# Hybrid decoder trunk: the stationary activation tiles stored interleaved, with gaps between the tensors

## The reference

```python
h = h + gated_deltanet(rms_norm(h, ...), gdn_w_in, gdn_conv_w, ..., gdn_w_out)   # 2048 -> 12352 -> 2048
h = h + swiglu_ffn(rms_norm(h, ...), w_gate_up, w_down)                          # 2048 -> 2 x 5632 -> 2048
shared_kv = nsa_shared_kv(h, kv_norm_g, kv_w, ...)                               # 2048 -> 3072
h = h + nsa_attention(rms_norm(h, ...), shared_kv, w_in, w_out)                  # 2048 -> 2096, 2048 -> 2048
h = h + swiglu_ffn(rms_norm(h, ...), w_gate_up, w_down)
return rms_norm(h, final_norm_g)
```

## Time and profile before

| | |
|---|---|
| time, median of three | 2800.06 us |
| profiled execution | 2803.94 us |
| its span | 2802.1 us |
| granted clock of TensorE, mean | 0.995 |
| PE busy | 2739.6 us, 13456 matmuls |
| weight loads busy | 2282.1 us, 13456 |
| DVE busy | 2219.6 us |
| ACT busy | 1648.4 us |
| read from HBM | 489.86 MB, 176 GB/s over the span |

### The profile page before, as it was taken

The page is one execution under the profiler, slowest core; times in us unless marked ns, Lnnn a source line. Parts: engine busy times, 40 slices in busy tenths (PEclk is TensorE's granted clock), DMA queues, the critical chain, the costliest instruction groups (busy, mean ns, idle before and its releaser), DMA issues.

```text
span 2802.1 us, 40252 instructions
## 1 busy us (share of the span) xinstructions
PE 2739.6 (98%) x13456; PEld 2282.1 (81%) x13456; DVE 2219.6 (79%) x2727; ACT 1648.4 (59%) x2184; POOL 31.0 (1%) x30
## 2 busy tenths in 40 slices
PE   8999999999988999999999999999999999999998
PEld 6878888888877888888888888888887888888887
DVE  5867877878767788888888876557677888888887
ACT  6766767667665555555555555554555555555554
POOL 0000000000000000000000000000000000000000
PEclk9999999999999999999999999999999999999999
DMA  6534444445433566656666656643345666656664
GB/s 239 181 124 153 159 144 163 156 149 167 158 105 113 166 210 199 198 185 203 198 198 203 198 172 224 222 135 114 106 158 188 207 199 200 199 184 200 198 201 166
DMA packets 135097, 493.23 MB, mean 176 GB/s; under 512 B 15009, under 2 KB 15329, under 8 KB 134625
## 3 DMA queue, kind: packets, MB, share of 16 engines
q1 hardware_dynamic: 133776, 487.82, 52.8%
q10 hardware_dynamic: 1232, 4.23, 0.4%
HBM read 489.86 MB, written 2.13 MB: 176 GB/s over the span
## 4 chain that ended last, share of the span: by engine, by line
PE 65%; issue 29%; DVE 3%; ACT 2%; DMA 1%; POOL 0%; POOLq 0%; DVEq 0%; SPq 0%; ACTq 0%
PE ACC L733 10%; PE ACC L735 10%; PE ACC L734 10%; PE SIDE L943 7%; PE SIDE L944 7%; PE SIDE L945 7%; PE ACC L943 3%; PE ACC L944 3%; PE ACC L945 3%; PE SIDE L741 2%; DVE W_LO L1627 1%; DMA RAW<-stream 1%; PE SIDE L1138 1%; ACT W_HI L1194 0%; ACT WORK L1587 0%
## 5 line engine op out<-in xcount | busy, mean ns | idle before, releaser
L1627 DVE TENSOR_TENSOR W_LO<-RAW,W_HI 128x1024 fp32r<-128x1024 f32 x424 | 511.6, 1222 | 268.9 <-ACT W_HI L1194 265.8
L1194 ACT ACTIVATE W_HI<-RAW 128x1024 fp32r<-128x1024 f32 x424 | 443.3, 1057 | 217.5 <-PE ACC L735 183.8
L1436 ACT ACTIVATE W_HI<-WORK 128x1024 fp32r<-128x1024 f32 x320 | 325.4, 1031 | 345.8 <-PE SIDE L945 232.7
L733 PE MATMUL ACC<-W_HI,X_HI 128*128 128x512 f32 x1216 | 491.2, 404 | 17.7 <-DVE W_LO L1627 17.6
L735 PE MATMUL ACC<-W_HI,X_LO 128*128 128x512 f32 x1216 | 477.6, 393 | 0.0
L734 PE MATMUL ACC<-W_LO,X_HI 128*128 128x512 f32 x1216 | 476.7, 392 | 0.0
L1878 DVE TENSOR_TENSOR W_LO<-WORK,W_HI 128x1024 fp32r<-128x1024 f32 x300 | 364.5, 1221 | 119.0 <-ACT W_HI L1436 116.3
L1436 ACT ACTIVATE W_HI<-RAW 128x1024 fp32r<-128x1024 f32 x328 | 314.8, 980 | 237.0 <-PE ACC L735 141.6
L733 PE MATMUL ACC<-W_HI,A_HI 128*128 128x512 f32 x928 | 370.3, 399 | 0.7 <-issue 0.7
L735 PE MATMUL ACC<-W_HI,A_LO 128*128 128x512 f32 x928 | 362.7, 391 | 0.0
L734 PE MATMUL ACC<-W_LO,A_HI 128*128 128x512 f32 x928 | 362.2, 390 | 0.0
(11 more groups left out here) (363 smaller groups left out, 3798.7 us busy)
## 6 DMA issues: line engine op xcount, KB each, us to landing
RAW<-stream SPq DMA_DIRECT2D x752, 512.0 KB, 4.6
WORK<-stream SPq DMA_DIRECT2D x160, 512.0 KB, 4.8
WORK<-gdn_rows ACTq DMA_DIRECT2D x8, 512.0 KB, 6.2
WORK<-xt SPq DMA_DIRECT2D x4, 512.0 KB, 9.3
H<-x SPq DMA_DIRECT2D x2, 1024.0 KB, 13.6
out<-WORK SPq DMA_DIRECT2D x4, 512.0 KB, 3.5
WORK<-tails SPq DMA_DIRECT2D x2, 512.0 KB, 10.8
WORK<-gfin SPq DMA_DIRECT2D x1, 1024.0 KB, 6.6
```

Source lines behind the costliest of these rows:

```text
L733: nc.tensor.matmul(dst, hi[:, at:at + P], wh, start=first and h % 2 == 0 and q == 0, stop=False)
L1194: nc.scalar.activation(W_HI[:, h % WS, :], raw_piece(h), ACT.Copy).then_inc(hi_ready, 1)
L1436: nc.scalar.activation(dst, src, ACT.Copy).then_inc(hi_ready, 1)
L1627: nc.vector.tensor_tensor(W_LO[:, h % WS, :], raw_piece(h), W_HI[:, h % WS, :].bitcast(f32), SUB).then_inc(lo_ready, 1)
```

## The change

The two token tiles of a k-tile are stored interleaved: column 2i + t of the 256 columns of a k-tile holds token i of token tile t. A stationary tile is then 128 words at a step of two. All that write such tiles (ACT for the high part, DVE for the low part) write with a step of two and read the transposed source in its old order; DVE reads the high part with a step of two. The tail matmuls read X as the moving operand in two runs with a step of two, so that their output has the old order. The token sums read X in the new order and write contiguous tiles as before.

Three unused tensors of 16 words (64 bytes per partition) lie before A_HI, before B_HI and after H. X then starts at a multiple of 4 KB from the weights W_HI and W_LO, A at 64 bytes more, B and H at 128 bytes more, and TR and all that follows at 192 bytes more. The scaled form of `act_in_vector` becomes two operations, one for each token tile.

```diff
@@ build: the tensors in SBUF
-        A_HI, A_LO, B_HI, B_LO = (sb(n, [P, CHK * SEQ], f32r) for n in ("A_HI", "A_LO", "B_HI", "B_LO"))
+        sb("GAP_A", [P, 16])
+        A_HI, A_LO = (sb(n, [P, CHK * SEQ], f32r) for n in ("A_HI", "A_LO"))
+        sb("GAP_B", [P, 16])
+        B_HI, B_LO = (sb(n, [P, CHK * SEQ], f32r) for n in ("B_HI", "B_LO"))
         H = sb("H", [P, NT, DM])
+        sb("GAP_Z", [P, 16])
@@ new helpers
+        def paired(ap):
+            return ap.rearrange("p (u i t) -> p u t i", t=NT, i=P)
+        def plain(ap):
+            return ap.rearrange("p (u t i) -> p u t i", t=NT, i=P)
+        def stationary(buf, at):
+            first = at // SEQ * SEQ + at % SEQ // P
+            return buf[:, first:first + SEQ - 1:NT]
@@ products (up_products and last_products likewise)
-                    nc.tensor.matmul(dst, hi[:, at:at + P], wh, start=first and h % 2 == 0 and q == 0, stop=False)
-                    nc.tensor.matmul(dst, hi[:, at:at + P], wl, start=False, stop=False)
-                    m = nc.tensor.matmul(dst, lo[:, at:at + P], wh, start=False, stop=last and h % 2 == 1 and q == 1)
+                    x_hi_, x_lo_ = stationary(hi, at), stationary(lo, at)
+                    nc.tensor.matmul(dst, x_hi_, wh, start=first and h % 2 == 0 and q == 0, stop=False)
+                    nc.tensor.matmul(dst, x_hi_, wl, start=False, stop=False)
+                    m = nc.tensor.matmul(dst, x_lo_, wh, start=False, stop=last and h % 2 == 1 and q == 1)
@@ tail_tensor
-                nc.tensor.matmul(SIDE[0][:, 0:SEQ], both, X_HI[:, at], start=kt == 0, stop=False)
-                m = nc.tensor.matmul(SIDE[0][:, 0:SEQ], both, X_LO[:, at], start=False, stop=kt == KT - 1)
+                dst = plain(SIDE[0][:, 0:SEQ])
+                nc.tensor.matmul(dst, both, paired(X_HI[:, at]), start=kt == 0, stop=False)
+                m = nc.tensor.matmul(dst, both, paired(X_LO[:, at]), start=False, stop=kt == KT - 1)
@@ norm_scalar (first_scalar, act_in_scalar and the casts of hid_t likewise)
-                i = nc.scalar.activation(X_HI[:, kt * SEQ:(kt + 1) * SEQ], SIDE[r % 2][:, q * SEQ:(q + 1) * SEQ],
+                i = nc.scalar.activation(paired(X_HI[:, kt * SEQ:(kt + 1) * SEQ]),
+                                         plain(SIDE[r % 2][:, q * SEQ:(q + 1) * SEQ]),
@@ norm_vector (first_vector and hid_lo likewise)
-                i = nc.vector.scalar_tensor_tensor(X_LO[:, at], SIDE[r % 2][:, q * SEQ:(q + 1) * SEQ],
+                i = nc.vector.scalar_tensor_tensor(paired(X_LO[:, at]), plain(SIDE[r % 2][:, q * SEQ:(q + 1) * SEQ]),
...
-                                                   X_HI[:, at].bitcast(f32), MUL, SUB)
+                                                   paired(X_HI[:, at].bitcast(f32)), MUL, SUB)
@@ act_in_vector
-            hi = to_hi[:, :].bitcast(f32)
+            hi, lo, full = paired(to_hi[:, :].bitcast(f32)), paired(to_lo[:, :]), plain(SIDE[p][:, :])
             if gain is None:
-                i = nc.vector.tensor_tensor(to_lo[:, :], SIDE[p][:, :], hi, SUB)
+                i = nc.vector.tensor_tensor(lo, full, hi, SUB)
             else:
-                i = nc.vector.scalar_tensor_tensor(to_lo[:, :], SIDE[p][:, :], gain, hi, MUL, SUB)
+                for t in range(NT):
+                    i = nc.vector.scalar_tensor_tensor(lo[:, :, t, :], full[:, :, t, :], gain, hi[:, :, t, :], MUL, SUB)
@@ token_sums
-            x4 = x_sum.rearrange("p (j a n) -> p a j n", j=4, a=4)
-            a11, a21, a12, a22 = (x4[:, i] for i in range(4))
+            x4 = x_sum.rearrange("p (j q n t) -> p q t j n", j=4, q=2, t=NT)
+            a11, a21, a12, a22 = (x4[:, q, t] for q in range(2) for t in range(NT))
```

More of the change, by code:

```diff
@@ L953, in up_products @@
             kt = 4 * j + (2 if kind[0] == "p" else 0)
-            a11, a21, a12, a22 = (tuple(b[:, at:at + P] for b in (X_HI, X_LO))
+            a11, a21, a12, a22 = (tuple(stationary(b, at) for b in (X_HI, X_LO))
                                   for at in ((kt + q) * SEQ + t * P for q in range(2) for t in range(NT)))
@@ L982, in last_products @@
                         wh, wl = (b[:, h % WS, q * COLS:(q + 1) * COLS] for b in (W_HI, W_LO))
-                        m = three(dst, B_HI[:, at:at + P], B_LO[:, at:at + P], wh, wl, h == 30 and q == 0, h == 31 and q == 1)
+                        m = three(dst, stationary(B_HI, at), stationary(B_LO, at), wh, wl, h == 30 and q == 0, h == 31 and q == 1)
                     if t:
@@ L1221, in first_scalar @@
                 at = slice(kt * SEQ, (kt + 1) * SEQ)
-                i = nc.scalar.activation(X_HI[:, at], XT[:, at], ACT.Copy, scale=PRM[:, A_GAIN + kt:A_GAIN + kt + 1])
+                i = nc.scalar.activation(paired(X_HI[:, at]), plain(XT[:, at]), ACT.Copy, scale=PRM[:, A_GAIN + kt:A_GAIN + kt + 1])
             i.then_inc(x_hi, 1)
@@ L1239, in act_in_scalar @@
             act.wait_ge(side_full[p], n)
-            nc.scalar.activation((to or A_HI)[:, :], SIDE[p][:, :], ACT.Copy, scale=gain).then_inc(act_hi, 1)
+            nc.scalar.activation(paired((to or A_HI)[:, :]), plain(SIDE[p][:, :]), ACT.Copy, scale=gain).then_inc(act_hi, 1)
         def pairs64(buf):
@@ L1476, in ffn_scalar @@
                     act.wait_ge(side_out[0], ph.after("hid_t", 0))
-                    nc.scalar.activation(A_HI[:, :], hid_t, ACT.Copy).then_inc(act_hi, 1)
+                    nc.scalar.activation(paired(A_HI[:, :]), plain(hid_t), ACT.Copy).then_inc(act_hi, 1)
             for k in range(0 if first else 4):
@@ L1486, in ffn_scalar @@
                         act.wait_ge(side_out[0], ph.after("hid_t", it))
-                        nc.scalar.activation(B_HI[:, :], hid_t, ACT.Copy).then_inc(act_hi, 1)
+                        nc.scalar.activation(paired(B_HI[:, :]), plain(hid_t), ACT.Copy).then_inc(act_hi, 1)
                 for half in range(2):
@@ L1633, in first_vector @@
                 at = slice(kt * SEQ, (kt + 1) * SEQ)
-                i = nc.vector.scalar_tensor_tensor(X_LO[:, at], XT[:, at], PRM[:, A_GAIN + kt:A_GAIN + kt + 1],
-                                                   X_HI[:, at].bitcast(f32), MUL, SUB)
+                i = nc.vector.scalar_tensor_tensor(paired(X_LO[:, at]), plain(XT[:, at]),
+                                                   PRM[:, A_GAIN + kt:A_GAIN + kt + 1],
+                                                   paired(X_HI[:, at].bitcast(f32)), MUL, SUB)
             i.then_inc(x_first, 1)
@@ L1955, in hid_lo @@
                 dve.wait_ge(act_hi, n + hi0)
-                nc.vector.tensor_tensor(lo[:, :], hid_t, hi[:, :].bitcast(f32), SUB).then_inc(act_lo, 1)
+                nc.vector.tensor_tensor(paired(lo[:, :]), plain(hid_t), paired(hi[:, :].bitcast(f32)), SUB).then_inc(act_lo, 1)
             for e in range(0 if first or final_ else 24):
```

## The result

The kernel with the change takes 2854.75 us (median of 4, 2854.14 to 2857.69) beside 2800.29 for the kernel before on the same chip (4 runs, 2799.73 to 2801.63). The ratio is 1.0196, with a 95% interval from 1.0178 to 1.0214: slower by 2.0%, 54.5 us. The prediction said 2714 us and faster.

The account below looks back on a forecast made before the run. PE was taken as the bound: number of matmuls times step. From 2803.9 us (profiled execution), minus 89 for the shorter step, plus 3 for strided operations and tail, came 2718; against the median 2714 us, range 2685 to 2915.

Parts of the forecast that it names:

- What the step is made of: Each 512-column fp32r matmul: 226.8 ns were 213.3 of streaming plus the moving words' read stream meeting the weight load's.
- Part (1): Stationary tiles of X, A, B at every second word: 9552 matmuls step at 216 ns, saving 89 us, 76 to 103.
- The end of 213.3: Lower limit of the step of the 9552 matmuls with strided stationary tiles: it can't go below 213.3 ns.
- The end of 237.9: Upper limit of that step: the load may fetch twice as many pieces, doubling the excess of 11.1 to 237.9 ns.
- arriving share: How much step saving reaches the span: all 49 us in FFN, three quarters of 54 us elsewhere, 40 us.
- Part (2): ACT and DVE writing X, A, B, and DVE reading the high half, at every second word: 2 us, ends 0 and 8.
- Part (3): Scaled split of the attention input as two operations of 512 elements: 747 each against 1278, +0.22 us eight times; nothing.
- Part (4): The 64 matmuls of 256 columns at L769/L770 stream X at every second word: 1 us, from 0 to 7.
- Part (5): The three gaps shifting A by 64 bytes, B and H by 128, what follows by 192: put at nothing.
- twice the collisions: Rival at each of the 9552 steps: load collides twice as often, step 237.9 ns, +106 us, 2909; chance 0.23.
- The distance decides: Rival: X at distance 0 keeps its step, 2769 (chance 0.09), or collides permanently, 2840 (0.06); the other tiles gain.
- no change: Rival: the excess is sequencing between load and matmul that doesn't see addresses; 2803 us, chance 0.10.

Follow-up runs that it names:

- the streams: No kernel computation: segments of 48 identical matmuls on one core, stationary tile contiguous or at every second word, at various distances from W; 590.76 us in all.

## Why the prediction was wrong, point by point

*What bounds the kernel*: right. The steps of PE times their count give what was measured.

*What the step is made of*: here the prediction failed, before any edit was priced. It read 226.8 ns as 213.3 of streaming plus collisions with the load, which end when the two streams advance equally fast, and took L901 and L793 for signs of it. L901 was no fit: the words are plain fp32, and plain fp32 steps by 429.2 for 1024 cycles with its stationary tile contiguous or at every second word. L793 (6 ns over with 32 columns loaded and 128 moving) differs from the large matmul in both numbers, and isn't in proportion to the load either, since a quarter of the columns has half of the excess. The prediction gave the drop to the load; with 32 columns loaded and 512 moving the excess is 18.3 ns, and with 1 column 18.2, so it came with the fewer moving columns. The third sign, the 232 ns after an interruption, did show that the stream has a state, but it was taken to be a contact with the load.

*Part (1), 216 ns and 89 us*: the term that failed. "Two streams that meet once are pushed apart and stay apart" made the step 216; it became 233.3, 230.1 and 231.4, and no distance brings every second word under 230. The load was not what spoilt it: at every second word it still fits into a step of 120 ns under 256 columns, so its addresses can advance about as fast as was meant (1024 bytes in 120 ns beside the moving tile's 2048 in 213), and the step under 512 columns grew all the same. The 216 had the sign wrong. The end of 213.3 was far off: the lowest of all arrangements tried, contiguous at a distance of 0 modulo 256 bytes, is what the kernel had. The end of 237.9 held, but it was the price of a rival that the streams refute; that 2855 lies inside the range is owed to that rival, and is luck. Of the arriving share nothing was tested as it was meant, a saving; the longer steps arrived nearly in full (56 us of PE's work, 51 of span).

*Part (2), 2 us*: DVE's bound of 22 us from L2047 was far too wide, stride two costs it nothing; ACT's "nothing", from L1300, is 92 ns per 1024 words, all hidden. *Part (3)*: right, 742 ns each. *Part (4), 1 us of 0 to 7*: 7.0; the argument that the load's pace covers half the stream overlooked that a halved moving stream (256 columns now step by 229 ns) covers the load instead. *Part (5), nothing*: wrong by itself, 19.4 us when made alone. The ground given was the compression's stationary tiles, which start at changing multiples of 480 bytes and keep 119 ns; but those matmuls move 256 columns, and the step of 512 did change with the place.

*The rivals*: "twice the collisions" (2909) had a step of 237.9 in every place and put TR/UR at 227; none is seen. "The distance decides" gave 2840 with X colliding, nearest to 2855, and its sign was on record: X and A at different steps. Its mechanism held in half: the distance does decide, but all the families lose. The rule of independent read ports, "no change", had the load right and the result wrong: the Trainium skill (TensorE: Matmul & The Clock Gate, What happens when you issue a matmul) says that the load takes nothing from the running matmul. The trace agrees in that a load of one column frees nothing (231.5 ns); it disagrees in that the place of the stationary tile moves the step by 6.7 ns.

*What stays open*: why the fp32r stream steps by more than 213.3 ns at all, and how the places of the two tiles choose the step. That the places do it is shown; by what contact is not. The steps after an interruption cost X some 1.4 ns a matmul in the mean (228.1 over 226.7), 9 us in all; nothing was tried against them. No arrangement beat the kernel before; the 256-byte gaps equal it.

## What to carry to other kernels

Before an excess over the streaming time is put down to a neighbour, find rows that differ in one thing: same type, same moving columns, another load. Where matmuls of 512 fp32r columns are the bound, look at the distance of the stationary tile from the moving one modulo 256 bytes: 0 gave the lowest step (with the moving tile 16 bytes off it didn't), and a stray buffer of 64 bytes cost this kernel 2%. Measure such a step in a stream by itself before a whole kernel is laid out by it.

## What the runs showed of the hardware that was not expected

- Moving fp32r words: 226.7 ns for 512 columns at best, 229 to 234.3 at the other distances tried from 16 to 192 bytes (228.3 at 240, 233.3 at 248 and 252); plain fp32 214.6 per 512 cycles, bf16 215.8.
- The step repeats with 256 bytes of distance (256 as 0, 384 as 128; gaps of 256 bytes in the kernel cost nothing). Both tiles shifted together by 32, 64 or 128 bytes keep 226.7, shifted by 16 they go to 231.1.
- A stationary tile at every second word steps by about 213 ns with 128 columns moving (112 contiguous), but by 120.0 with 256 moving, as contiguous. Under 512 moving columns its loads are recorded with 193 to 197 ns (188 contiguous), and at every fourth word with 309. A moving tile at every second word runs at half pace (451 ns for 512).
- Every second word costs DVE nothing in writing and reading (1220 ns for 1024, 1219 before) and ACT 9% in these writes (1136 beside 1044).
